# One level of Strassen's algorithm in most projections of the first block, and its y kept in DRAM

## The reference

```python
xn = _rmsnorm(h, norm_w)
proj = xn @ w_in        # q, k, v_m, o_m, z_m, i, f, u_g, v_g, z_g
q, k = silu(causal_conv(concat(q, k)))          # 8 heads of 128
hm = mlstm(q, k, v, log_i, log_f)               # 8 heads, v of 256
hm = hm * rsqrt(mean(hm * hm, -1) + EPS)
y_m = hm * mlstm_norm_w * sigmoid(o_m) * silu(z_m)
vg = layernorm(gelu(v_g))                       # 8 heads of 256
sv = w_spatial @ vg + b_spatial                 # within 128 tokens
y_g = gelu(u_g) * sv * silu(z_g)
h = h + concat([y_m, y_g]) @ w_out              # 4096 -> 2048
```

## Time and profile before

| | |
|---|---|
| median of 3 runs | 3402.8 us (3401.52 to 3403.43) |
| span of the profiled execution | 3400.8 us |
| PE busy | 3293.3 us (97%) |
| DVE busy | 1741.2 us (51%) |
| ACT busy | 1367.7 us (40%) |
| DMA moved | 325.42 MB, mean 96 GB/s |

### The profile page before, as it was taken

One profiled execution on the slowest core, in us unless ns is written; L12 is line 12 of the kernel. 1 busy time (PEld: TensorE's weight loads), 2 busy tenths in 40 slices (PEclk: granted clock), 3 DMA queues, 4 the chain that ended last, 5 costly groups with the idle time before them and its releaser, 6 DMA issues.

```text
span 3400.8 us, 53969 instructions
## 1 busy us (share of the span) xinstructions
PE 3293.3 (97%) x19734; PEld 2902.3 (85%) x19734; DVE 1741.2 (51%) x2525; ACT 1367.7 (40%) x2173; POOL 306.7 (9%) x291
## 2 busy tenths in 40 slices
PE   8999999999999999899969999999997999999997
PEld 7889888888888888788868999999997888888786
DVE  6332333434444434424685555556557465556647
ACT  5332332333333333323244444555226355545424
POOL 1000000000000000000000412431000033313000
PEclk9999999999999999999989999999998999999998
DMA  6332332323232322422234222221433422222422
GB/s 196 99 90 83 99 92 83 100 84 105 80 105 80 102 83 83 141 95 88 89 100 144 69 76 76 75 70 57 162 99 103 134 70 77 72 76 63 153 89 87
DMA packets 367638, 325.42 MB, mean 96 GB/s; under 512 B 23616, under 2 KB 363224, under 8 KB 365840
## 3 DMA queue, kind: packets, MB, share of 16 engines
q1 hardware_dynamic: 352064, 290.00, 28.0%
q10 hardware_dynamic: 11280, 19.25, 1.6%
q0 software_dynamic: 4176, 14.55, 1.3%
HBM read 306.66 MB, written 17.07 MB: 95 GB/s over the span
## 4 chain that ended last, share of the span: by engine, by line
PE 52%; DVE 4%; ACT 2%; issue 1%; DVEq 1%; ACTq 0%
PE ps L534 15%; PE ps L535 14%; PE ps L536 14%; PE ps L862 2%; PE ps L903 1%; DVE w_low L1551 1%; DVE residual L1800 1%; PE ps L540 1%; PE ps L541 1%; PE ps L542 0%; PE ps L849 0%; PE ps L877 0%; PE ps L934 0%; PE ps L910 0%; PE ps L881 0%
## 5 line engine op out<-in xcount | busy, mean ns | idle before, releaser
L534 PE MATMUL ps<-x_high,w_high 128*128 128x512 f32 (+3 forms) x4736 | 1641.8, 347 | 69.9 <-DVE w_low L1551 22.3
L535 PE MATMUL ps<-x_low,w_high 128*128 128x512 f32 (+3 forms) x4736 | 1606.9, 339 | 0.0
L536 PE MATMUL ps<-x_high,w_low 128*128 128x512 f32 (+3 forms) x4736 | 1601.3, 338 | 0.0
L1551 DVE TENSOR_TENSOR w_low<-w_raw,w_high 128x1024 fp32r<-128x1024 f32 x540 | 656.2, 1227 | 1019.0 <-ACT w_high L1030 991.9
L534 PEld LDWEIGHTS ps<-x_high,w_high 128*128 128x128 f32 x4736 | 897.6, 190 | 183.9 <-issue 79.6
L535 PEld LDWEIGHTS ps<-x_low,w_high 128*128 128x128 f32 x4736 | 897.6, 190 | 106.0 <-issue 7.2
L536 PEld LDWEIGHTS ps<-x_high,w_low 128*128 128x128 f32 x4736 | 896.5, 189 | 98.8
L1030 ACT ACTIVATE w_high<-w_raw 128x1024 fp32r<-128x1024 f32 x540 | 569.1, 1057 | 713.4 <-PE ps L536 572.1
L540 PE MATMUL ps<-w_high,x_high 128*128 128x256 f32 x1184 | 332.3, 281 | 3.5 <-DVE w_low L1551 2.7
L541 PE MATMUL ps<-w_high,x_low 128*128 128x256 f32 x1184 | 332.6, 281 | 0.0
L542 PE MATMUL ps<-w_low,x_high 128*128 128x256 f32 x1184 | 332.6, 281 | 0.0
(11 more groups left out here) (351 smaller groups left out, 2504.2 us busy)
## 6 DMA issues: line engine op xcount, KB each, us to landing
w_raw<-in_w_in SPq DMA_DIRECT2D x784, 256.0 KB, 3.1
w_raw<-in_w_out SPq DMA_DIRECT2D x280, 256.0 KB, 2.9
residual<-residual_stream ACTq DMA_DIRECT2D x8, 1056.0 KB, 12.3
residual_stream<-y_layer ACTq DMA_DIRECT2D x2, 2176.0 KB, 10.5
x_natural<-in_x SPq DMA_DIRECT2D x4, 1024.0 KB, 9.1
x_feature_major<-x_stage POOLq DMA_DIRECT2D x4, 1024.0 KB, 6.9
gate_bc<-gate_rows POOLq DMA_DIRECT2D x8, 512.0 KB, 4.5
acc<-x_feature_major POOLq DMA_DIRECT2D x1, 4096.0 KB, 13.7
```

The lines of the kernel that those rows point to most:

```text
L534: pe.matmul(dst, wh[:, j, kt, wc], xh[:, k, tok], start=first, stop=False)
L535: pe.matmul(dst, wh[:, j, kt, wc], xl[:, k, tok], start=False, stop=False)
L536: return pe.matmul(dst, wl[:, j, kt, wc], xh[:, k, tok], start=False, stop=last)
L1551: dve.tensor_tensor(wl[:, j], raw[:, j], f(wh[:, j]), ALU.subtract).then_inc(lo_ready, 1)
```

## The change

Units of gating heads 3 to 8 (18 of them) and of all mLSTM heads (32) are computed by one level of Strassen's algorithm in Winograd's form. The features (16 tiles), tokens (512) and columns (256) are each cut in halves. Seven products of 8 feature tiles, 128 columns and 256 tokens take the place of eight. Each product has three matmuls per feature tile, so a unit is 7 x 8 x 3 = 168 matmuls with 256 moving columns. The first two gating heads (PLAIN) stay as they were. The sums of activation blocks (S1 to S4) are built once, on DVE, in the second gating head, and split into high and low by ACT and DVE.

Per unit DVE now also makes four sums of weight blocks (`sums_13`, `sum_2`, `sum_4`) and combines products from PSUM (`out_11`, `out_12`, `out_22`, 128x256 each); ACT copies three partial products (`keep_p1`, `keep_u2`, `keep_q5`) and the fourth corner. There are seven high and seven low blocks of 128x1024 instead of four. The raw weights have one buffer for a unit, in a top and a bottom half of 1 MB. Every `low_block` waits for its `high_block`.

```diff
+            def load_blocks(s, col, pair=None, first=False):
+                for i, landed in ((0, in_top), (1, in_bot)):
+                    sp.wait_ge(lo_ready, done(s - 1, 6 if first else 4 + i))
+                    for r in range(2):
...
+            def sums_13(s):
+                dve.drain()
+                dve.wait_ge(in_top, 32 * s + 32)
+                dve.tensor_tensor(wt[:], w11, w12, ALU.add).then_inc(w_summed, 1)
+                dve.drain()
+                dve.wait_ge(in_bot, 32 * s + 32)
+                dve.scalar_tensor_tensor(w12, w12, -1.0, w22, ALU.mult, ALU.subtract).then_inc(w_summed, 1)
...
+            def out_22(s, banks, dst):
+                dve.wait_ge(pq_ok, 2 * s + 2)
+                dve.wait_ge(piece_used, done(s, B_S3))
+                dve.tensor_tensor(dst, pq[:], ps[:, banks[0], 0:SH], ALU.subtract).then_inc(c22, 1)
```

(B_S3 and B_S4 are blocks 4 and 5 of a unit, counted from 0, so the top half is loaded after the low part of S3 and the bottom half after that of S4.) On PE, per block:

```diff
+                    if i == B_A12:
+                        pe.wait_ge(c12, s + 1)
+                    if i == B_S3:
+                        pe.wait_ge(u2_ok, s + 1)
+                    if i == B_S4:
+                        pe.wait_ge(pq_ok, 2 * s + 2)
+                        pe.wait_ge(s_low, 8)
+                    if i == B_A22:
+                        pe.wait_ge(c22, s + 2)
+                    pe.wait_ge(lo_ready, done(s, i))
```

The PE's block order is A11, A12, S2, S1, S3, S4, A22. DVE's order in a unit of an mLSTM head (the gating heads' is the same but for `out_22`, which always stands before the low part of A11, and `out_12`, before that of A12):

```diff
+                    low_block(t, B_S3, slot(4))
+                    e0()
+                    before()
+                    out_11(t, banks, t0[:, 0:SH])
+                    low_block(t, B_S4, slot(5))
+                    e1()
+                    low_block(t, B_A22, slot(6))
+                    e2()
...
+                    if early:
+                        out_22(t, banks, t1[:, SH:S])
+                    sums_13(t + 1)
+                    low_block(t + 1, B_A11, slot(7))
+                    if not early:
+                        out_22(t, banks, t1[:, SH:S])
+                    sum_2(t + 1)
+                    low_block(t + 1, B_A12, slot(8))
+                    e3()
+                    out_12(t, banks, t1[:, 0:SH])
+                    low_block(t + 1, B_S2, slot(9))
+                    e4()
+                    low_block(t + 1, B_S1, slot(10))
+                    sum_4(t + 1)
+                    end()
...
+                body(0, crq[:, 3:3 + S], crk[:, 3:3 + S], e4=lambda: conv(kc, crk, 0, H), end=lambda: conv(qc, crq, 1, 0))
+                body(1, vf[:, 0, :], vf[:, 1, :], before=lambda: dve.wait_ge(y_st, 16 * H + 16 * h), e2=p_args, early=True,
+                     e4=lambda: p_tiles(0, 2), end=lambda: p_tiles(2, ST))
+                body(2, og[:, 0, :], og[:, 1, :], e3=denominators)
+                body(3, zz[:, 0, :], zz[:, 1, :], before=lambda: dve.wait_ge(v_tr, h + 1), e0=mean_squares, e1=roots, early=True,
+                     end=gated, stop=last)
```

In the second gating head DVE has this between the low parts of u's weights and the batch statistics:

```diff
+                if ending:
+                    dve.wait_ge(wst_ok, 1)
+                    sum_parts(sf[B_S3], ((a21[0], None), (a11[0], ALU.subtract), (a21[1], ALU.add), (a11[1], ALU.subtract)))
+                    dve.wait_ge(at_ok, 1)
+                    dve.wait_ge(gr_stored, 16)
+                    sum_parts(sf[B_S1], ((a21[0], None), (a22[0], ALU.subtract), (a21[1], ALU.add), (a22[1], ALU.subtract)))
+                    dve.drain()
+                    sum_parts(sf[B_S2], ((sf[B_S3], None), (a22[0], ALU.subtract), (a22[1], ALU.subtract)))
                 dve.wait_ge(evac, 2 * U + 2)
+                deviations(h, lambda i: vg[:, i, :])
```

More of the change, by code:

```diff
@@ L158, in program @@
         big = r0.at
[L161 to L166, removed]
         xs = nc.alloc_sbuf_tensor_at("x_scaled", [P, ST, D], F32, offset=big)
+        ym_at = big + KT * S * 4
         xn = nc.alloc_sbuf_tensor_at("x_natural", [P, ST, D], F32, offset=ym_at)
+        work = ym_at + KT * S * 4
         rp = Region(work)
@@ L383, in _ @@
                 for n, c in enumerate((C_V, C_O, C_Z)):
-                    load(U + 1 + n, cols(w_in, c + DV * h))
+                    load_blocks(S_MLSTM + 4 * h + 1 + n, c + DV * h)
+            passed_blocks = NBLOCK
+            for j in range(4):
+                sp.wait_ge(lo_ready, done(S_END - 1, 4 + j // 2))
+                for i in range(2):
+                    sp.dma_start(raw[:, j, 2 * i:2 * i + 2, :], cols(w_out, 0, row=KT)(j, slice(2 * i, 2 * i + 2))).then_inc(raw_full[j], 16)
@@ new lines, in _ @@
+            sp.wait_ge(y_st, 16 * H)
+            for j in range(4):
+                sp.wait_ge(piece_used, done(S_END - 1, B_S2 + j // 2))
+                sp.dma_start(yst[:, 4 * j:4 * j + 4, :], y_gd[:, 4 * j:4 * j + 4, :]).then_inc(part_in[j], 16)
+            for d in range(1, 3):
+                load(U_OUT_G + d, cols(w_out, 256 * d, row=KT))
+            sp.wait_ge(x_ready, 2 * KT)
+            sp.wait_ge(y_st, 32 * H)
+            for j in range(4):
+                sp.dma_start(yst[:, 4 * j:4 * j + 4, :], y_md[:, 4 * j:4 * j + 4, :]).then_inc(part_in[j], 16)
@@ new lines, in _ @@
+            for h in range(PLAIN):
+                U = U_SGU + 3 * h
+                unit_tokens(U, 0, 0, tok1)
+                unit(U + 1, 0, after=(lambda: mix(h, 6, 4), None))
+                unit(U + 2, 0)
+                if h == 0:
+                    pe.wait_ge(g_m, 1)
+                    for i in range(ST):
+                        last = pe.transpose(ps[:, 7, i * H:(i + 1) * H], gz[0:H, i * P:(i + 1) * P], ident[0:H, 0:H])
+                    last.then_inc(at_tr, 1)
+            pe.wait_ge(at_ok, 1)
@@ L712, in squares @@
+                def squares(i):
+                    if i != B_A11:
+                        return
                     pe.wait_ge(sq_sum, h + 1)
                     pe.matmul(ps[:, 7, :], ones[:], sq[:, 0, :], start=True, stop=True).then_inc(ms_mm, 1)
-                unit(U, 0)
-                unit_tokens(U + 1, 0, 0, tok1, after=(scores, None))
-                unit(U + 2, 0, after=(values, None))
-                unit(U + 3, 0, after=(squares, None))
+                for u, hook in enumerate((None, scores, values, squares)):
+                    unit_blocks(s + u, banks_mlstm(u), [(7 * u + i) % 4 for i in range(7)], hook)
@@ new lines, in head @@
+                body(3, end=True, **z_rows)
+                for j in range(3):
+                    high(U_OUT_G, j)
+                act.wait_ge(piece_used, done(S_END - 1, B_S4))
+                for j in range(2):
+                    act.wait_ge(part_in[j], 32)
+                    fill_piece(j, yst, slice(0, S))
+                high(U_OUT_G, 3)
+                act.wait_ge(piece_used, done(S_END - 1, B_A22))
+                for j in range(2, 4):
+                    act.wait_ge(part_in[j], 32)
+                    fill_piece(j, yst, slice(0, S))
@@ L1183, in _ @@
+                second_row(s + 3, zz, ACT.Silu)
+                corner(s + 3, banks_mlstm(3), zz[:, 0, SH:S], ACT.Silu)
+            passed_blocks = NBLOCK
+            with act.Fori(0, H - 1) as h:
+                head(h, False)
+            head(H - 1, True)
+            act.wait_ge(ym_done, H + 1)
+            for U0 in (U_OUT_G, U_OUT_M):
+                first = 16 if U0 == U_OUT_M else 0
                 with act.Fori(0, 6 if first else 7) as d:
@@ L1760, in fill_piece @@
                        .then_inc(x_ready, 2)
+            passed_blocks = NBLOCK
+            with dve.Fori(0, H - 1) as h:
+                head(h, False)
+            head(H - 1, True)
             def spread(k, c=slice(0, L)):
```

795 lines of the change are left out of this document (570 added, 225 removed).

## The result

The changed kernel takes 3410.36 us (median of 16 executions, 3407.3 to 3412.08), the kernel before 3402.44 us (16, 3400.84 to 3403.58). The ratio is 1.0023, interval 1.0016 to 1.003: **slower by 7.9 us**, 0.2% and clear of noise, where 16 had been forecast.

What follows compares the result with a forecast made beforehand. PE bounded the kernel before; with the change, DVE's queue waiting on weight loads would pace mLSTM heads. 3400.8 + 26 - 25 + 20 - 5 = 3416.8 us, median 2.0 above: 3419, range 3385 to 3445.

Steps and rivals of the forecast that it cites:

- What bounds the kernel now, and PE's new floor: PE bounds; 256-column matmuls at 0.118 us put gating heads at 62.6 and mLSTM heads at 88.8, 111 us gained at best.
- DVE's new load: In an mLSTM head, DVE needs 15.1 us per unit plus 21, so 81 of PE's 88.8 us.
- the loop through the load: mLSTM heads: DVE's queue waits for the next unit's weights in the only buffer; 101 us a head, +26 us in all.
- The collision: mLSTM heads: POOL issues 1 MB just as unit 1's weights are requested; 3.5 us, of which 1.5 charged.
- factor of eight: mLSTM heads: 3.3 us more per head, multiplied by eight heads, gives +26 us.
- The gating heads: Six gating heads at 65.0 us instead of 69.2: -25 us (-40 to -13).
- The second gating head: Activation sums on DVE delay normalised values, stalling PE 17 us; first Strassen unit 4 us late: +20 (+12 to +26).
- The seam: Before the output product: y_g's first pieces are split beside A22, replacing PE's 9.31 us idle: -5 us (-9 to +3).
- Rest: Second half's y lands far ahead; repeated last unit and second block as before: 0.
- PE-bound: Rival, chance 0.10: the bottom half lands before DVE asks for it and DVE's 81 us fit; 3304 us.
- Half the wait: Rival, chance 0.17: operations overlap better, mLSTM heads take 96 and gating heads 63.5; 3367 us.
- The clock too: Rival, chance 0.13: half clock after each stall costs PE 2 to 4 us, mLSTM heads take 104; 3443 us.

Runs made afterwards that it cites:

- the quarter loads: Changed kernel with each Strassen weight DMA after the first unit moving a quarter of its bytes (outputs wrong); span 3353.6 us against 3410.2.
- the last kernel: Changed kernel with strip loads, activation sums moved, `out_22` ahead of `sums_13` and POOL's megabyte after unit 1's landing; 3329.72 us, 0.9783 of the kernel before.
- the kernel with POOL moved: Changed kernel with POOL's y store and `gate_bc` load held until unit 1's weights of the next head have landed; span 3386.4 us against 3410.2.
- the early `out_22`: Changed kernel with `out_22` ahead of `sums_13` in all four units of an mLSTM head; 3408.07 us, span 3406.6 against 3410.2.

## Why the prediction was right or wrong

- **What bounds the kernel now, and PE's new floor:** held. 256-column matmuls kept their 0.118 us; PE is busy 91.3 and 63.1 us in the heads, and the quarter loads let the gating heads run at exactly 62.6. Of the forecast 88.8 for an mLSTM head, the last kernel shows 89.14 busy, at clock 1.00.
- **DVE's new load:** 75.7 us busy instead of 81. The low parts start 1.14 us apart instead of 1.17, and a sum behind its drain 1.31 after the start of the operation before it, instead of 1.40. Part of the rest is that the 81 counted drains as load, which the busy time leaves out. DVE's timeline of the changed kernel, in unit 1:

```profile
942.33 1.23 DVE L1988 SCALAR_TENSOR_TENSOR w_raw_blocks<-w_raw_blocks 128x1024 f32<-128x1024 f32 x1 [1.37 <-DMA w_raw_blocks<-in_w_in]
943.47 1.22 DVE L1979 TENSOR_TENSOR w_low_blocks<-w_raw_blocks,w_high_blocks 128x1024 fp32r<-128x1024 f32 x1
944.78 1.23 DVE L1993 TENSOR_TENSOR w_raw_blocks<-w_sum,w_raw_blocks 128x1024 f32<-128x1024 f32 x1
```

- **The step that failed, the loop through the load:** +12.8 us instead of +26, and this is where the forecast's excess lay. Part of the mechanism held: `out_22` releases PE, before A22 of unit 0, and DVE's idle is ended by the weights' DMA, 13.2 us of it in a head. What failed is that the prediction let DVE's loop pace all four units. It had PE idle for 12 us of a head of 101 and busy 88.8. The trace has PE idle for 8.4 us, 8.25 of them at one load, and busy 91.3 without a gap from there to the next head's stall, while DVE's `out_22` waits for PE in units 1 and 3. A head is thus PE's own work plus one wait, not the sum of four loops.
- **The same step, its terms:** from low part of S3 to low part of S3 the units took 28.6, 22.7, 21.7 and 26.7 us, against 26.6 + 1.5, 23.9, 22.1 and 26.9. Three terms were too large: the landing of a unit, 8.3 to 8.5 instead of 8.9 (three units, 1.5 us; `load_blocks` issues 4 DMAs where the earlier trace rows has 8, but that this is the reason was not shown); three sums a unit in the loop (12 by 0.09, 1.1 us); five low parts (20 by 0.03, 0.6 us). That brings 99.5 to 96.3, and the kernel with POOL moved shows 96.4 to 97.1. The agreement is in part luck: the measured units 1 and 3 hold waits for PE, which this sum does not have. Two terms were too small. The collision costs 2.8 and not the 1.5 charged: I had taken part of POOL's transfers to run ahead of the load, but y's store is issued 0.66 us before the first weights and `gate_bc` 0.27 us after them. And the half clock stood at nothing in the sum, where PE at full clock would have been busy some 89 us instead of 91.3. The steady heads come to 99.9 instead of 101, 7.5 us in all.
- **The same step, its factor of eight:** the first head takes 95.2 us, with a stall of 3.9 us: no mLSTM head's gating precedes it, and its low part of S3 ends 8.2 us after the head's start where the others' takes 11.6 (905.28 less 893.68). Its load of unit 1 took 9.9 us and not 11.2, with the store of y and `gate_bc` issued 4 us apart. I multiplied a steady head by eight where seven are steady; that was 5.8 us. The two together are the 13 us. The other stages came out 6.6 us dearer than forecast, so the total looks better than the loop's own term did: luck, as far as the total goes.
- **The gating heads:** 65.2, 65.4, 65.2, 65.1 and 64.9 us for the last five against 65.0; -24.2 against -25.
- **The second gating head:** a stall of 15.0 instead of 17, with the releaser named. The clock was granted at half after it, so 16 mixing matmuls took 3.78 us instead of the 1.95 of the earlier trace rows; the forecast had left that out. The stage starts 19.0 us late and its first unit loses 3.9, the 4 forecast: 22.8 against +20.
- **The seam:** PE's gap is 1.89 instead of the 9.31 of the earlier trace rows; gaps of 0.89 and 0.61 follow before later pieces of y_g, and one of 1.50 before a low part of the weights: -4.1 against -5.
- **Rest:** +2.1 against 0. This stage's work is the same in both kernels, and 2.1 us is within what executions of one kernel differ by.
- **The rivals.** *PE-bound* fell: the bottom half does not land before DVE asks for it. *Half the wait* named the right direction of the error, but its reason, operations that overlap better, gave only 1.7 us of a head; its 96 would have needed no collision. *The clock too* held in its mechanism and not in its size: in the changed kernel the granted clock is 0.50, the 1.2 GHz level, in 919.5 to 923, after the stall of 8.25 us, and PE is busy 90.8 to 92.1 us in the heads, where the last kernel has 89.14 at full clock. The chain that ended last runs on PE alone from 919.53 to 987.81 us, half clock included, so part of these some 2 us is in the head's time. How much, no run of the changed kernel shows; the last kernel, with and without the half clock, shows 1.3 to 1.9 us a head, not 3. Nor did it take an idle stretch of about 9 us, or "somewhat shorter": 5.17 us were enough with the early `out_22`, and 2.82 us in the last kernel, in two heads and not in four others.

```profile
918.50:922.00 3.50, 3.46 (x16) 3.46 (x17) 3.42 (x4) 2.08 (x3) 0.00 (x0) 0.50 0.00 0
```

  By the rule cited in the prediction (the Trainium skill, TensorE: Matmul & The Clock Gate, part on the HAM clock gate) an idle PE falls to half clock; the trace agrees.

In short, the sign was right because the stall before A22 of unit 0 and the one in the second gating head were. The loop's term was twice too large: a chain of DVE work was taken to pace four units where one load holds PE and PE's own work sets the rest, three small durations in it were set a little high, and the first head was taken for a steady one.

## What to carry to other kernels

When work is added to an engine that seems to have room, don't stop at its busy share: write down its queue between the release of a buffer and the operation that the bounding engine waits for, and put into it the landing of the load that stands there. Ask for a single buffer's parts as each comes free, put a short result that another engine needs ahead of any wait for a load, and keep other queues' bulk transfers off the one load that has no slack: here this turned a change that lost 0.2% into one that gains 2.2%. In the forecast, do it unit by unit for both engines: where the other engine is later, your loop does not set the time. Count the first pass of a loop apart. And hold a stall against the waits of the engine that ends it: here it was their sum plus 0.65 to 0.76 us in four kernels, which tells landing from backlog at once.

## What the runs showed of the hardware

- 2 MB of weights in 4 DMAs of 512 KB landed in 8.3 to 8.5 us, some 250 GB/s; with 1 MB issued by POOL within 1 us of them, in 11.2 us.
- After idle stretches of 5.2, 8.3 and 15.0 us PE's granted clock was 0.50 in the 3.5 to 4.2 us cut out behind them. In the kernel with strips and POOL's wait it fell to 0.50 behind stalls of 2.82 us in two heads, which took 94.0 and 93.6 us, and stayed 1.00 behind stalls of 2.76 to 2.84 us in four, which took 92.1 to 92.3.
- A stall of PE behind DVE can be read as DVE's waits and a rest: in 21 of the heads of three kernels it was DVE's waits for the load plus 0.63 to 0.67 us, in seven of a fourth plus 0.74 to 0.76.
- A DVE operation behind a drain started 0.09 us after the end of a 1024-column one (943.47 and 1.22 to 944.78), where the earlier trace rows had shown 0.17 behind a 512-column one.
